# Gated delta rule: applying T once to the corrected values instead of to values and keys apart

## The reference

```
tri = where(strict, beta_i * kk * decay, 0) + eye
rhs = concatenate([v * beta, k * (beta * exp(G))])
u, w = triangular_solve(tri, rhs)          # u = T (v beta), w = T (k beta e^G), T = tri^-1
def step(S, inp):
    v_new = u_c - w_c @ S
    o = qd_c @ S + qk_c @ v_new
    S = cd_c * S + kd_c^T @ v_new
```

## Time and profile before

| | |
|---|---|
| time, median of 3 runs | 1437.5 us (1435.81 to 1437.81) |
| the profiled execution, its own time | 1436.72 us |
| span of the trace | 1434.9 us, 18557 instructions |
| PE busy | 1391.0 us (97%) |
| DVE busy | 748.4 us (52%) |
| ACT busy | 606.9 us (42%) |
| the eight heads | from about 69 to 397 us, 41 us each |

### The profile page before, as it was taken

How to read it: one execution, slowest core, us unless ns; L and a number is a source line. 1 busy time by engine, 2 the same in 40 slices (tenths; PEclk the granted TensorE clock), 3 DMA queues, 4 the chain that set the end, 5 groups by cost and what they waited for, 6 DMA issues and landing times.

```text
span 1434.9 us, 18557 instructions
## 1 busy us (share of the span) xinstructions
PE 1391.0 (97%) x6729; PEld 1139.5 (79%) x6729; DVE 748.4 (52%) x1088; ACT 606.9 (42%) x961; POOL 24.3 (2%) x19
## 2 busy tenths in 40 slices
PE   6599999999989999999999999999999999999998
PEld 3488888888768888888887777777888888888886
DVE  7667666666464334343456543447643343434555
ACT  4446555655444223142346445544442232323342
POOL 6000000000000000000000000000000000000000
PEclk9799999999999999999999999999999999999999
DMA  4222322312133333333233312112433333333323
GB/s 148 59 60 60 73 59 73 60 52 63 63 90 101 103 88 103 101 90 102 88 91 120 115 57 59 44 54 65 161 95 105 95 103 88 92 103 96 88 88 103
DMA packets 42338, 124.09 MB, mean 86 GB/s; under 512 B 3952, under 2 KB 12720, under 8 KB 41776
## 3 DMA queue, kind: packets, MB, share of 16 engines
q1 hardware_dynamic: 33472, 117.08, 27.2%
q10 hardware_dynamic: 8816, 6.33, 2.5%
HBM read 119.17 MB, written 4.23 MB: 86 GB/s over the span
## 4 chain that ended last, share of the span: by engine, by line
PE 92%; DVE 3%; ACT 2%; DMA 1%; issue 1%; POOL 1%; SPq 0%; ACTq 0%; DVEq 0%; POOLq 0%
PE acc L306 26%; PE acc L308 25%; PE acc L307 25%; PE ps L421 2%; PE ps L443 2%; PE ps L643 2%; PE ps L627 1%; PE ps L659 1%; DVE work L1333 1%; POOL work L1265 1%; PE ps L401 1%; DMA work<-rows 1%; DVE wl L281 1%; PE ps L671 0%; PE ps L464 0%
## 5 line engine op out<-in xcount | busy, mean ns | idle before, releaser
L306 PE MATMUL acc<-xh,wh 128*128 128x512 f32 x976 | 401.8, 412 | 0.0
L308 PE MATMUL acc<-xh,wl 128*128 128x512 f32 x976 | 381.5, 391 | 0.0
L307 PE MATMUL acc<-xl,wh 128*128 128x512 f32 x976 | 380.7, 390 | 0.0
L275 ACT ACTIVATE wh<-raw 128x1024 fp32r<-128x1024 f32 x208 | 217.4, 1050 | 179.4 <-DMA raw<-in_weights 152.3
L281 DVE TENSOR_TENSOR wl<-raw,wh 128x1024 fp32r<-128x1024 f32 x208 | 254.6, 1224 | 71.2 <-ACT wh L275 68.0
L306 PE MATMUL acc<-yh,wh 128*128 128x512 f32 x656 | 259.8, 396 | 19.0 <-DVE yl L1786 12.0
L308 PE MATMUL acc<-yh,wl 128*128 128x512 f32 x656 | 257.3, 392 | 0.0
L307 PE MATMUL acc<-yl,wh 128*128 128x512 f32 x656 | 257.3, 392 | 0.0
L308 PEld LDWEIGHTS acc<-xh,wl 128*128 128x128 f32 x976 | 183.3, 188 | 39.7
L306 PEld LDWEIGHTS acc<-xh,wh 128*128 128x128 f32 x976 | 184.1, 189 | 37.6 <-issue 4.9
L307 PEld LDWEIGHTS acc<-xl,wh 128*128 128x128 f32 x976 | 184.0, 189 | 35.7 <-issue 4.1
(11 more groups left out here) (239 smaller groups left out, 1207.4 us busy)
## 6 DMA issues: line engine op xcount, KB each, us to landing
raw<-in_weights SPq DMA_DIRECT2D x208, 512.0 KB, 3.5
work<-rows ACTq DMA_DIRECT2D x16, 256.0 KB, 6.8
h<-in_xT SPq DMA_DIRECT2D x4, 512.0 KB, 6.6
proj<-work ACTq DMA_DIRECT2D x2, 1024.0 KB, 4.2
work<-proj SPq DMA_DIRECT2D x2, 1024.0 KB, 7.4
outT<-h SPq DMA_DIRECT2D x8, 256.0 KB, 2.5
cst<-in_cst SPq DMA_DIRECT2D x1, 640.0 KB, 4.0
work<-in_pT SPq DMA_DIRECT2D x1, 512.0 KB, 5.9
```

Of the source, the lines that this page charges most:

```text
L275: nc.scalar.activation(wh[u.const % 4][:], raw[u.const % 2][:], ACT.Copy).then_inc(hi_done, 1)
L306: nc.tensor.matmul(dst[:], hi, mh[:, k, :], start=(n == 0), stop=False)
L307: nc.tensor.matmul(dst[:], hi, ml[:, k, :], start=False, stop=False)
L308: mm = nc.tensor.matmul(dst[:], lo, mh[:, k, :], start=False, stop=(n == KT - 1))
```

## The change

w is no longer computed. With u - w S = T (vb - kbeta S), where kbeta are the keys scaled with beta e^G, a new step ks(c) multiplies the raw keys (`kcur`, a copy that ACT makes, since the next head's keys overwrite `kc`) with the state into bank ps3. DVE (`correct(c)`) multiplies that by minus beta e^G (table 2, whose sign is now turned in the prelude) and adds it to `vb`. Then v(c) applies T once. The product S times qd moves from v(c) to ks(c). ACT's copies to `kb` and `nw` are gone, its copy to `kcur` is new, and the convolution input of v (`take(2)`) moves behind vn(1). ktr moves from w to v(0). The list has 24 steps with new FILL tables.

```diff
@@ -199,7 +199,7 @@
                                            sem("vb_done"), sem("qd_done"))
         t_d, tt_d, x_d, xs_d, tx_d = (sem("t_updated"), sem("tt_updated"), sem("x_done"), sem("x_copied"),
                                       sem("tx_done"))
-        w_d, nw_d, v_d, vn_d, su_d, s_d, o_d = (sem("w_done"), sem("nw_done"), sem("v_done"), sem("vn_done"),
+        kcur_d, ks_d, v0_d, v_d, vn_d, su_d, s_d, o_d = (sem("k_kept"), sem("state_keys"), sem("v_corrected"), sem("v_done"), sem("vn_done"),
                                                 sem("state_mm"), sem("s_done"), sem("o_done"))
         osq_d, oss_d, oln, ors, o1_d, yb_d, yh_d, yl_d = (sem("o_squared"), sem("o_sums"), sem("o_ln"), sem("o_rstd"),
                                                    sem("o_scaled"), sem("y_done"), sem("yh_done"), sem("yl_done"))
@@ -389,8 +389,6 @@
 
         def pe_qk(pe, h):
             pe.wait_ge(q_silu, h + 1)
-            if not isinstance(h, int) or h > 0:
-                pe.wait_ge(nw_d, h)
             for c in range(C):
                 last = nc.tensor.matmul(ch(ps[1], c), ch(kc, c), ch(qc, c), start=True, stop=True)
             last.then_inc(qk_d, 1)
@@ -449,30 +447,27 @@
                     last.then_inc(tx_d, 1)
                 return step
 
-            def w():
-                pe.wait_ge(tt_d, i * 6)
-                for c in range(1, C):
-                    last = nc.tensor.matmul(ch(ps[1], c), ch(kb, c), ch(TT, c), start=True, stop=True)
-                last.then_inc(w_d, 1)
-                if project:
-                    pe_ktr(pe, i)
+            def ks(c):
+                def step():
+                    if c == 1:
+                        pe.wait_ge(kcur_d, i)
+                    pe.wait_ge(s_d, b * 3 + c)
+                    nc.tensor.matmul(ch(ps[3], c), ch(kcur, c), S, start=True, stop=True).then_inc(ks_d, 1)
+                    if c == 1:
+                        pe.wait_ge(qd_d, i)
+                    nc.tensor.matmul(ch(ps[5], c), S, ch(qd, c), start=True, stop=False)
+                return step
 
             def v(c):
                 def step():
                     if c == 0:
+                        pe.wait_ge(tt_d, i * 6)
                         pe.wait_ge(vb_d, i)
-                    last = nc.tensor.matmul(ch(ps[3], c), ch(TT, c), ch(vb, c), start=True, stop=(c == 0))
-                    if c > 0:
-                        if c == 1:
-                            pe.wait_ge(nw_d, i)
-                        pe.wait_ge(s_d, b * 3 + c)
-                        last = nc.tensor.matmul(ch(ps[3], c), ch(nw, c), S, start=False, stop=True)
-                    last.then_inc(v_d, 1)
-                    if c > 0:
-                        if c == 1:
-                            pe.wait_ge(qd_d, i)
-                        nc.tensor.matmul(ch(ps[5], c), S, ch(qd, c), start=True, stop=False)
+                    else:
+                        pe.wait_ge(v0_d, b * 3 + c)
+                    nc.tensor.matmul(ch(ps[3], c), ch(TT, c), ch(vb, c), start=True, stop=True).then_inc(v_d, 1)
                     if c == 0 and project:
+                        pe_ktr(pe, i)
                         pe_kk(pe, i)
                 return step
@@ -495,13 +490,13 @@
                 pe_norm(pe, i)
 
             return ([x(1), tx(1), vtr] + [s for n in range(2, 7) for s in (x(n), tx(n))]
-                    + [w] + [s for c in range(C) for s in (v(c), os(c))] + ([] if project else [norm]))
-
-        FILL = [2, 2, 0, 2, 2, 2, 2, 2, 2, 2, 2, 2, 1, 1, 1, 1, 1, 1, 1, 1, 1, 1]
+                    + [v(0), os(0)] + [s for c in range(1, C) for s in (ks(c), v(c), os(c))] + ([] if project else [norm]))
+
+        FILL = [2, 2, 0, 2, 2, 2, 2, 2, 2, 2, 1, 2, 1, 0, 1, 1, 1, 1, 1, 1, 1, 1, 1, 1]
         assert sum(FILL) == 4 * KT
 
         OUT_AHEAD = ((4, 5), (5,), (5,), (), (), (), (2,), (2,))
-        LAST_FILL = [1, 1, 0, 1, 1, 1, 1, 1, 1, 2, 2, 1, 1, 1, 1, 1, 1, 1, 1, 1, 1, 2, 4]
+        LAST_FILL = [1, 1, 0, 1, 1, 1, 1, 1, 1, 2, 1, 1, 1, 1, 1, 1, 1, 1, 1, 1, 1, 1, 1, 1, 4]
         assert sum(LAST_FILL) == 4 * (KT - 1)
 
         def pe_out_steps(pe):
@@ -890,6 +885,8 @@
                 act.wait_ge(cwc_d, i + 1)
                 if n < 2:
                     act.wait_ge(qk_d, i)
+                if n == 0:
+                    act.wait_ge(kcur_d, i)
                 if n == 1:
                     act.wait_ge(qd_d, i)
                 if n == 2:
@@ -948,14 +945,14 @@
                 act_rows(act, i)
             act.wait_ge(tcur_d, i)
             if past:
-                act.wait_ge(w_d, b)
                 act.wait_ge(su_d, b * 3)
-            for c in range(C):
-                if c < C - 1:
-                    nc.scalar.activation(ch(kd, c), ch(ps[2], c), ACT.Copy, scale=tc(3, c))
-                if c > 0:
-                    ins = nc.scalar.activation(ch(kb, c), ch(ps[2], c), ACT.Copy, scale=tc(2, c))
+            for c in range(C - 1):
+                ins = nc.scalar.activation(ch(kd, c), ch(ps[2], c), ACT.Copy, scale=tc(3, c))
             ins.then_inc(ktok_d, 1)
+            if past:
+                act.wait_ge(ks_d, b * 3)
+            act.wait_ge(k_silu, i)
+            nc.scalar.activation(kcur[:, P:], kc[:, P:], ACT.Copy).then_inc(kcur_d, 1)
             act.wait_ge(q_silu, i)
             if past:
                 act.wait_ge(osum_d, b)
@@ -990,15 +987,14 @@
                 nc.scalar.activation(eg, grow, ACT.Exp).then_inc(eg_d, 1)
                 silu(kc, 3, k_silu)
                 silu(qc, 6, q_silu)
-            act_nw(act, i)
             if project:
                 act_ksq(act, i)
             vn_copy(0)
-            if project:
-                take(2)
             act_gs(act, i)
             for c in range(1, C):
                 vn_copy(c)
+                if project and c == 1:
+                    take(2)
             if project:
                 silu(vc, 9, v_silu)
             act.preload_act_table_set(LN_EXP)
@@ -1016,12 +1012,6 @@
 
             act.wait_ge(yb_d, i)
             nc.scalar.activation(yh[:, bass.ds(i - 1, 1), :], yb.unsqueeze(1), ACT.Copy).then_inc(yh_d, 1)
-
-        def act_nw(act, i):
-            act.wait_ge(w_d, i)
-            if not isinstance(i, int) or i > 1:
-                act.wait_ge(v_d, (i - 1) * 4)
-            nc.scalar.activation(nw[:, P:], ps[1][:, P:], ACT.Copy, scale=-1.0).then_inc(nw_d, 1)
 
         def act_gs(act, i):
             if not isinstance(i, int) or i > 1:
@@ -1300,7 +1290,8 @@
 
             def s3():
                 dve.wait_ge(g_act, 8)
-                nc.vector.tensor_tensor(tabs[:, 64:96], tabs[:, 64:96], tabs[:, 32:64], ALU.mult).then_inc(g_dve, 1)
+                nc.vector.scalar_tensor_tensor(out=tabs[:, 64:96], in0=tabs[:, 64:96], scalar=-1.0, in1=tabs[:, 32:64],
+                                               op0=ALU.mult, op1=ALU.mult).then_inc(g_dve, 1)
                 dve.wait_ge(g_pe, 4)
                 dve.wait_ge(g_dve, 9)
                 nc.vector.tensor_copy(W(23)[0:64, 0:P], ps[4][0:64, 0:P]).then_inc(g_dve, 1)
@@ -1522,15 +1513,24 @@
                     dve.wait_ge(s_d, b * 3 + c)
                     nc.vector.scalar_tensor_tensor(out=S, in0=S, scalar=tc(4, c), in1=ps[4][:, 0:P],
                                                    op0=ALU.mult, op1=ALU.add).then_inc(s_d, 1)
+            def correct(c):
+                dve.wait_ge(ks_d, b * 3 + c)
+                if c == 1:
+                    dve.wait_ge(vb_d, i)
+                nc.vector.scalar_tensor_tensor(out=ch(vb, c), in0=ch(ps[3], c), scalar=tc(2, c), in1=ch(vb, c),
+                                               op0=ALU.mult, op1=ALU.add).then_inc(v0_d, 1)
             state(0)
+            correct(1)
             if project:
                 next_pairs()
                 split_lo(dve, Unit(4, i, 4))
             state(1)
+            correct(2)
             if project:
                 next_ti()
                 next(v_taps)
             state(2)
+            correct(3)
             if project:
                 next(v_taps)
                 next(v_taps)
```

More of the change, by code:

```diff
@@ L164, in build @@
         TT0 = W(5)
-        Ti, TT, Xs, kb, kd, vb = W(16), W(17), W(18), W(19), W(20), W(21)
-        nw, qd, vn, eg, osq, yb = W(22), W(23), W(24), W(25), W(26), W(27)
+        Ti, TT, Xs, kd, vb = W(16), W(17), W(18), W(20), W(21)
+        kcur, qd, vn, eg, osq, yb = W(22), W(23), W(24), W(25), W(26), W(27)
         S = W(28)[:, 0:P]
```

## The result

The changed kernel takes 1439.64 us (median of 22 runs, 1438.09 to 1441.95); the kernel before, timed beside it, 1436.62 us (22 runs). The ratio is 1.0021, 95% interval [1.0015, 1.0028]: 3.0 us slower, after a forecast of 2.8 us (a median of 1440.3 us in a range of 1435.5 to 1444). The profiled execution took 1440.78 us, its span is 1439.0 us.

A forecast was written before the change was run, and what follows sets the result against it. PE's order of matmuls was taken to bound each head. Seven heads at -0.1 us, seven head starts at 2.45 and the last head at 0.4 gave +2.8 us: a 1440.3 us median, range 1435.5 to 1444.

The forecast's parts named there:

- What goes: PE in each of eight heads: the three products of w vanish, 0.66 us a head, 5.3 us in all.
- From v(0) to ks(1): PE's own work takes 3.56 us, state(0) allows ks(1) at 4.09: 0.53 us wait, plus 0.03 at the next start.
- The chunks: Three chunks of a head: correct hidden, each os load waits for vn, costing 0.03 us each, 0.09 us together.
- rival 2: Late loads cost their whole wait, a head's-start delay hits tx(1) and norm: 0.83 us more a head, 1446 us; chance 0.11.
- The end of a head: Taps of v behind correct(3) end later, delaying ACT: next head's norm waits 0.31 us, tx(1) 0.03; 0.34 us together.
- The last head: Its end hangs on v(3); one more k-tile before v(3) makes the last norm 0.4 us late, losing this head's gain.
- The sum: Seven heads -0.1 us, seven head starts 2.45 us, last head 0.4 us: +2.8 us in all.
- Rival 1: Waits stay hidden, matmul counts decide: 1433 us, faster; needs both waits under 0.25 us a head; chance 0.15.
- Rival 3: The split behind correct(1) holds up state(1), so ks(2) and the taps slip: 0.2 us more a head, 1441.7 us; chance 0.14.
- The extra 0.09 us behind `correct`: On DVE, if each operation waits for an empty pipe, correct(3) holds the taps 0.09 us longer; sum 0.6 us more.

The follow-up runs named there:

- w twice: The kernel before with its three products of w done twice; 1441.56 us, ratio to before 1.0039.
- all four edits: Changed kernel with vn(0) before the squares, state(0) before the Lt products, a tap before correct(3), another last-head fill; 1432.15 us, ratio to before 0.9969.
- the moved tap: Changed kernel with DVE doing the second tap of v between state(2) and correct(3) instead of behind correct(3); 1436.32 us, ratio to before 0.9995.
- the fill table: Changed kernel, last head only: one k-tile less before v(3), three instead of one behind os(3), three instead of four behind the norm; 1438.36 us, ratio 1.0014.

## Why the prediction was right

**What goes, 0.66 us a head.** Shown: w twice adds 0.66 us.

**From v(0) to ks(1), 0.53 + 0.03 us.** The place and the order of the waits were right: the squares, their sum, Lt, the copy. ks(1) came at 4.00 instead of 4.09 us, because a load that comes after its matmul was due starts together with it, not 0.08 us ahead: the loader's timeline of the changed kernel has

```profile
227.21 0.30 PEld L455 LDWEIGHTS ps<-work 128*128 128x128 f32 x2 [0.37 <-DVE work L1511]
```

and the matmul starts at 227.21 too. All the steps up to it are within 0.01 us of the forecast (Lt at 2.63, the copy from 3.67 to 3.95, the load at 4.00). What I put at 0.03 us, the next start, is 0.10 us after such a load. The two errors cancel, which is luck: 13.57 us from v(0) to x(1), forecast 13.58. The experiments add what my sum did not need: os(0)'s wait for vn lies inside this wait and costs 0.33 us by itself as soon as the other one is removed.

**The chunks, 0.09 us.** Three late loads, each 0.2 us by the loader's list and 0.03 us by the next start. The kernel with all four edits shows them by themselves. Its loader's list, 70 to 400 us, still has all 24 of them (three in each of eight heads) and os(0) of the last head, 4.9 us in total:

```profile
PEld ps L481 <- ACT work L902: 3.3, 17, 0.2
...
PEld ps L482 <- ACT work L902: 1.6, 8, 0.2
```

But from ks(1) to x(1) it takes 9.45 us, and PE's own starts add up to 9.38 (twice 1.14 + 0.92 + 1.14, and 2.98): 0.07 us for three loads. That dismisses the first half of rival 2, which asked for 0.51 us. It also fits the whole head, 0.61 us shorter than before, where w alone is 0.66 us.

**The end of a head, 0.34 us, measured 0.42 us.** The cause is shown by moving one tap. x(2) comes 0.09 us later and the norm 0.23 us more (1.13 instead of 0.89 to 0.90 us behind x(2)), 0.32 us together, as forecast with 0.34. What the sum left out is the start behind the late norm: the k-tile follows it after 0.56 us in the changed kernel and after 0.47 us before, the same drawn-out start as behind ks(1). In PE's timeline of the changed kernel and then of the kernel before (to be read with the norm at 242.99 and, in the earlier trace rows, at 238.64):

```profile
243.55 0.80 PE L306 MATMUL acc<-xh,wh 128*128 128x512 f32 x1
```

```profile
239.11 0.80 PE L306 MATMUL acc<-xh,wh 128*128 128x512 f32 x1
```

This is also what became of rival 2's second half: the delay does hit twice, at tx(1) (0.09 us, where I had 0.03) and at the norm, but with 0.42 us in all and not 0.75.

**The last head.** Forecast 0.41 us for its start and 0.4 us for its end; measured 0.69 us together (35.81 to 36.50), of which the moved tap gives back 0.43 us and the fill table 0.59 us. Its start measured 0.42 us (6.03 instead of 5.61 us from x(1) to the first norm), so the term for its end was too large, 0.27 us and not 0.4; why is not shown. From v(3) to the norm both kernels take 3.48 us (394.49 to 397.97, and the earlier trace rows), so the end hangs on v(3) as forecast, and that the gain of this head is lost was right.

**The sum.** Per head -0.66 + 0.56 + 0.09 + 0.34 = +0.33 us forecast, 41.57 - 41.22 = +0.35 us measured. That is as close as it is because errors of up to 0.1 us a head in single terms have opposite signs. The line I drew for rival 2, 0.02 us above my sum, is reached by this number and was drawn too near to decide anything; the single terms decide it, as said above. Rival 1 (waits hidden) failed where it had to: the two sums of waits are 1.0 us a head (0.61 us from v(0) to x(1), 0.42 us behind it), not under 0.25. It is also what the kernel with all four edits does: the head shrinks by 0.61 us and the time by 4.5 us of the 5.3. Rival 3 did not come about: the split did hold up state(1), which started at 229.93 and not 0.42 us behind os(1) at 229.80, but it ended at 230.27 and ks(2) followed without a wait, 1.17 us behind os(1). The extra 0.09 us behind `correct` did not come about either: correct at 234.20 lasts 0.35 us and the tap behind it starts at 234.47, 0.27 us later. I had read the Trainium skill (VectorE: DVE Perf Modes, section "The DRAIN you can't avoid") too briefly there: the section adds that a next operation that is not held back starts earlier, and the trace agrees with that.

## What to carry to other kernels

When a product is taken off the bound engine's list and a short step on another engine put in its place, look at what stood between the old steps as cover, and at what stands behind the new step in its engine's queue: here the link itself cost nothing, and the work queued behind it and in front of it cost more than the products were worth. Repairs have to be judged together, since a wait inside another shows no gain by itself. Three operations moved within two engines' orders, and one fill table, turned a loss of 3.0 us into a gain of 4.5 us.

## What the runs showed of the hardware

- In these traces a weight load that waited cost PE little as long as it started before its matmul was due: 0.20 us of waiting moved the next start from 0.22 to 0.25 us. Where the matmul itself was late, load and matmul started together (227.21) and the next start was 0.32 us away: 0.10 us on top of the lateness.
- The profiled execution of the changed kernel has a span 4.1 us longer than that of before, the medians differ by 3.0 us. By stretches the 4.1 us are 1.4 before the first x(1), 1.6 in the first head, 2.1 in the six heads after it, 0.7 in the last one and 1.6 less behind the last norm. That last stretch, which the change does not touch, took between 1040.8 and 1043.8 us in the ten profiles. The first head differs by its clock: PE had idled 15.9 us before it (14.3 us in the kernel before), and its clock was back at the full 2.4 GHz later. Windows of PE in the changed kernel (columns: stretch, length and busy time, granted clock, DMA share, GB/s):

```profile
69.00:71.00 2.00, 2.00 (x10) 0.50 0.30 77
71.00:73.00 2.00, 2.00 (x6) 0.50 0.19 58
73.00:75.00 2.00, 2.00 (x10) 0.56 0.70 209
75.00:77.00 2.00, 2.00 (x14) 1.00 0.16 64
```

and in the kernel before:

```profile
69.00:71.00 2.00, 2.00 (x9) 0.70 0.25 67
71.00:73.00 2.00, 2.00 (x14) 1.00 0.59 103
```

  At 1.2 GHz a k-tile matmul takes 0.43 us from start to start instead of 0.23. The changed kernel's first head lasted 43.39 us in this profile, the six variants with correct had 42.1 to 42.7 us, the one without it 43.3 us, the kernel before 41.84 us, and the same with w twice 43.9 us, of which its products are 0.66 us. Each of these is one execution. The first head's excess over the other heads of its kernel lies between 0.5 and 2.2 us, with no order that follows the edits, and only the other heads repeat, to 0.06 us.
